# Layer 0's adaLN products in a two-layer fp32 diffusion step: half of the weight units as split fp32r products, loads spread over the phase, six units in flight in place of four

## The reference, cut to what matters

```python
def ada_modulate(x, cond, w_ada, b_ada, norm_g):
    mod = jax.nn.silu(cond) @ w_ada + b_ada
    shift, scale, gate = jnp.split(mod[:, None, :], 3, axis=-1)
    h = rms_norm(x, norm_g) * (1 + scale) + shift
    return h, gate
...
out, k, v = run_mixer(layer, h, ...)     # h @ w_in, attention and gating, @ w_out
x = x + gate * out
```

## Time and profile before

| | us |
|---|---|
| median of 3 runs | 2793.45 (2782.55 to 2796.37) |
| the profiled execution | 2779.65 |
| its span in the trace | 2778.1 |
| PE busy in the span | 2555.4 (92%) |
| DVE busy | 1720.0 (62%) |
| ACT busy | 809.4 (29%) |
| start of the first projection product | 165.56 |

### The profile page before, as it was taken

One profiled execution on the slowest core, in us unless ns is written; L12 is line 12 of the kernel. 1 busy time (PEld: TensorE's weight loads), 2 busy tenths in 40 slices (PEclk: granted clock), 3 DMA queues, 4 the chain that ended last, 5 costly groups with the idle time before them and its releaser, 6 DMA issues.

```text
span 2778.1 us, 38161 instructions
## 1 busy us (share of the span) xinstructions
PE 2555.4 (92%) x12040; PEld 2009.0 (72%) x12040; DVE 1720.0 (62%) x3165; ACT 809.4 (29%) x1698; POOL 428.1 (15%) x481
## 2 busy tenths in 40 slices
PE   7999999998898899979999989999999999998995
PEld 1258877777777678868877777777777778777884
DVE  1335788877887547766356555665656656555776
ACT  2012232322222222222233333333333333332221
POOL 0000212211222010000122212222222211101001
PEclk8999999999999999989999999999999999999998
DMA  7745544444544455644422222232222322237555
GB/s 273 253 148 163 192 147 144 137 152 157 171 158 147 164 187 194 216 152 148 131 91 89 86 78 83 86 98 92 68 91 88 99 87 95 84 122 241 189 194 203
DMA packets 165601, 395.42 MB, mean 142 GB/s; under 512 B 15008, under 2 KB 15648, under 8 KB 160992
## 3 DMA queue, kind: packets, MB, share of 16 engines
q1 hardware_dynamic: 132304, 249.08, 28.6%
q0 software_dynamic: 33168, 144.72, 14.8%
HBM read 332.93 MB, written 63.18 MB: 143 GB/s over the span
## 4 chain that ended last, share of the span: by engine, by line
PE 61%; DVE 19%; DVEq 8%; issue 5%; ACT 4%; DMA 2%; ACTq 0%; POOL 0%; SPq 0%; POOLq 0%
PE ps L554 46%; DVE w_lo L1138 4%; PE ps L440 3%; PE ps L449 3%; DVE small L1026 3%; PE ps L583 3%; PE ps L458 3%; DVEq L1161 2%; DVE work L1043 2%; ACT w_hi L769 1%; PE ps L541 1%; DMA w_raw<-in_w_ada_dram 1%; DVE wT_lo L1018 1%; DVEq L1024 1%; DVEq L1048 1%
## 5 line engine op out<-in xcount | busy, mean ns | idle before, releaser
L554 PE MATMUL ps<-w_hi,hT_hi 128*128 128x512 f32 x2800 | 1145.4, 409 | 15.0 <-DVE stage L1155 7.1
L554 PE MATMUL ps<-w_hi,hT_lo 128*128 128x512 f32 x2800 | 1106.4, 395 | 0.0
L554 PE MATMUL ps<-w_lo,hT_hi 128*128 128x512 f32 x2800 | 1100.7, 393 | 0.0
L1138 DVE TENSOR_TENSOR w_lo<-w_raw,w_hi 128x512 fp32r<-128x512 f32 x560 | 406.2, 726 | 351.7 <-ACT w_hi L769 333.8
L554 PEld LDWEIGHTS ps<-w_hi,hT_lo 128*128 128x128 f32 x2800 | 530.7, 190 | 118.9
L554 PEld LDWEIGHTS ps<-w_hi,hT_hi 128*128 128x128 f32 x2800 | 533.3, 190 | 112.0 <-issue 13.6
L554 PEld LDWEIGHTS ps<-w_lo,hT_hi 128*128 128x128 f32 x2800 | 533.2, 190 | 91.9 <-issue 1.9
L769 ACT CAST w_hi<-w_raw 128x512 fp32r<-128x512 f32 x560 | 346.6, 621 | 487.3 <-PE ps L554 468.5
L1168 DVE SCALAR_TENSOR_TENSOR ada_sum<-w_raw,cond,ada_sum 128x512 f32<-128x512 f32 x480 | 366.8, 805 | 35.8 <-issue 10.1
L720 ACT ACTIVATE work<-ps,small 128x640 f32<-128x640 f32 (+1 forms) x200 | 141.9, 710 | 594.5 <-DVE small L1029 594.4
L440 PE MATMUL ps<-consts,work 128*128 128x128 f32 x768 | 133.9, 289 | 68.9 <-DVE q_low_lo L1018 19.7
(11 more groups left out here) (185 smaller groups left out, 2374.1 us busy)
## 6 DMA issues: line engine op xcount, KB each, us to landing
w_raw<-in_w_in_dram SPq DMA_DIRECT2D x216, 512.0 KB, 3.9
w_raw<-in_w_ada_dram SPq DMA_DIRECT2D x256, 256.0 KB, 3.0
z<-stage POOLq DMA_DIRECT2D x27, 1280.0 KB, 5.1
w_raw<-in_w_ada_dram SPq DMA_DIRECT2D x64, 512.0 KB, 4.7
w_raw<-in_w_out_dram SPq DMA_DIRECT2D x64, 512.0 KB, 4.2
work<-z POOLq DMA_DIRECT2D x72, 320.0 KB, 3.7
work<-o POOLq DMA_DIRECT2D x8, 1280.0 KB, 7.7
x<-stage POOLq DMA_DIRECT2D x7, 1280.0 KB, 11.7
```

The costliest lines, as they stand in the source:

```text
L554: last = nc.tensor.matmul(ps[:, t, :], x[:, kt, t * P:(t + 1) * P], w[:, kt % RING, :], start=(kt == 0 and i == 0), stop=(kt == KT - 1 and ...
L1138: nc.vector.tensor_tensor(w_lo[:, kt % RING, :], w_raw[:, w_at(c, kt), kt % 2, :], w_hi[:, kt % RING, :].bitcast(F32), ALU.subtract).then_ ...
```

## The change

Of the 64 units, the even ones (`SPLIT`) are now handled as the projections' weights are: ACT rounds each of the two tiles to `w_hi`, DVE makes `w_lo`, and PE multiplies both with weights that hold, in four columns for each tile, the rounded value and the remainder of both conditions (`cst`, in the place of `wT_lo`). PE makes four single-pass fp32r matmuls of them in place of two plain fp32 ones. The odd units (`PLAIN`) stay plain fp32, with weights from `oT`. The weights are 128 columns wide for both, of which four are used; the rows of the result are added pairwise by `sel_col` in `ada0_finish`. Twenty of the plain units (`ADA_B`) get two new buffers, in the places of `ws_t` and of the two rotation tables, which are loaded after the last unit (`tables_in`). The blocks of `x` are issued after 1, 5, 8 and 11 plain units (`X_AFTER`), and ACT squares a block six units later. The feed of tiles 0 to 11 starts at units 34, 44 and 54 (`FEED_AT`), one tile for each two units, with the split of the next even unit between two tiles. Two of the w units come before the last ada unit, six behind it.

```diff
+X_AFTER = (2, 10, 16, 22)
+FEED_AT = (34, 44, 54)
+SPLIT = [u for u in range(N_ADA0) if u % 2 == 0]
...
-W_UNIT_AFTER = {56: (0,), 60: (1,), 62: (2,), 64: (3, 4, 5, 6, 7)}
+W_UNIT_AFTER = {63: (0, 1), 64: (2, 3, 4, 5, 6, 7)}
...
+ADA_B = [u for u in range(60) if u % 6 in (1, 3)]
+FIRST_A = [x for x in FIRST if x[0] == "w" or x[1] not in ADA_B]
...
+        spare = [at[:, :].rearrange("p (k n) -> p k n", n=NC) for at in (ws_t, tables)]
...
+            setup_at = {n: (n - 2,) for n in range(2, 11)}
             for n, (kind, u) in enumerate(FIRST):
...
+                if kind == "ada" and u in ADA_B:
+                    b = ADA_B.index(u)
+                    if b >= 2:
+                        sp.wait_ge(ada0_taken, PLAIN.index(ADA_B[b - 2]) + 1)
+                        sp.sem_inc(raw_taken, 1)
+                    dst, landed = spare[b % 2], spare_landed[b % 2]
+                else:
+                    at = FIRST_A.index((kind, u))
+                    if at >= RAW:
+                        held, v = FIRST_A[at - RAW]
+                        if held == "w":
+                            sp.wait_ge(w_lo_ready, C_L0 * KT + 2 * v + 2)
+                        elif v in SPLIT:
+                            sp.wait_ge(w_lo_ready, 2 * SPLIT.index(v) + 2)
+                        else:
+                            sp.wait_ge(ada0_taken, PLAIN.index(v) + 1)
...
-            sp.wait_ge(ada0_taken, N_ADA0)
+            sp.wait_ge(ada0_taken, len(PLAIN))
             sp.sem_inc(raw_taken, 1)
+            for dst, src in ((rope_c, a["rope"][0, 0]), (rope_s, a["rope"][0, 1]), (ws_t[:, :], a["spatial_weights"])):
+                sp.dma_start(dst, src).then_inc(tables_in, 16)
...
             def ada0_unit(u):
...
-                    last = nc.tensor.matmul(ps[0:2, m % 2, :], cond2[:, kt, :], w_raw[:, n % RAW, k, :],
-                                            start=(kt == 0), stop=(kt == KT - 1))
+                    if u in SPLIT:
+                        tile = 2 * SPLIT.index(u) + k
+                        pe.wait_ge(w_lo_ready, tile + 1)
+                        for w in (w_hi, w_lo):
+                            last = nc.tensor.matmul(ps[:, m % 2, :], cst[:, kt * 4:kt * 4 + P], w[:, tile % RING, :],
+                                                    start=(kt == 0 and w is w_hi), stop=False)
+                        last.then_inc(*((acc_ready, 5) if tile % KT == KT - 1 else (w_used, 1)))
+                    else:
+                        last = nc.tensor.matmul(ps[:, m % 2, :], oT[:, kt * 4:kt * 4 + P], ada0_buffer(u)[:, k, :],
+                                                start=False, stop=(kt == KT - 1))
...
-                    beside.setdefault(16 * b + 19 + x, []).append(("turn", 4 * b + x))
-            beside[62] = [("turn", 12)]
+                    beside.setdefault(FEED_AT[b] + 2 * x, []).append(("turn", 4 * b + x))
+            beside.setdefault(63, []).append(("turn", 12))
...
+            # ACT
+            for u in range(N_ADA0):
+                if u in SPLIT:
+                    split_ada(u)
+                if u - 6 in X_AFTER:
+                    square_block(X_AFTER.index(u - 6))
...
+                for b, at in enumerate(FEED_AT):
+                    if u - at in (1, 3, 5, 7):
+                        feed_hi(0, 4 * b + (u - at) // 2)
...
+            # DVE
+            for u in range(N_ADA0):
+                if u in SPLIT:
+                    split_ada(u)
+                if u % 8 == 0 and u > 0:
+                    ada0_row(u // 8 - 1)
+                if u == 31:
+                    dve.wait_ge(sq_done, 4 * TT)
+                    row_norms(partial=True)
+                    feed_block(0, 0)
...
+                if u in (21, 37, 53):
+                    ada0_columns((21, 37, 53).index(u))
+                for b, at in enumerate(FEED_AT):
+                    if u - at in (1, 3, 5, 7):
+                        feed_mid(0, 4 * b + (u - at) // 2)
+                        feed_lo(0, 4 * b + (u - at) // 2)
+                    if u - at == 9:
+                        feed_block(0, b + 1)
+            for kt in range(4):
+                split_lo(C_L0, kt)
+            ada0_row(7)
             ada0_columns(3)
...
+                wait(ada0_taken, X_AFTER[b] // 2)
```

More of the change, by code:

```diff
@@ L204, in kernel_program @@
         raw_taken = sem("raw_taken")
+        spare_landed = [sem(f"spare_landed{i}") for i in range(2)]
+        tables_in = sem("tables_in")
         ada_landed = [sem(f"ada_landed{i}") for i in range(ADA)]
@@ L406, in w_at @@
         def w_at(c, kt):
-            if isinstance(c, int) and c == 0:
+            if isinstance(c, int) and c == C_L0:
                 return W_AT[kt // 2] % RAW
@@ L831, in _, with split_ada, square_block @@
             act.sem_inc(S[1].s_exp, 1)
-            for b in range(4):
+            def split_ada(u):
+                wait_ada0_landed(act, u)
+                for k in range(2):
+                    tile = 2 * SPLIT.index(u) + k
+                    wait_slot_used(act, tile // KT, tile % KT)
+                    nc.scalar.copy(w_hi[:, tile % RING, :], ada0_buffer(u)[:, k, :]).then_inc(w_hi_ready, 1)
+            def square_block(b):
                 act.wait_ge(x0_in[b], 32)
@@ L1326, in _ @@
-            for b in range(3):
-                ada0_columns(b)
-                for kt in range(4 * b, 4 * b + 4):
-                    feed_mid(0, kt)
-                    feed_lo(0, kt)
-                feed_block(0, b + 1)
-                ada0_row(2 * b + 2)
-                if b == 2:
-                    for kt in range(4):
-                        split_lo(C_L0, kt)
-                ada0_row(2 * b + 3)
+            nc.vector.tensor_scalar(small[:, 32:64], small[:, 32:64], 0.5, None, ALU.mult)
@@ new lines, in _ @@
+            dve.drain()
+            parts = cst[:, 0:4 * KT].rearrange("p (k q) -> p k q", q=4)
+            for k in range(2):
+                x = small[:, 32 + 16 * k:48 + 16 * k]
+                nc.vector.tensor_copy(cond4[:, :, 2 * k], x)
+                nc.vector.tensor_copy(oT[:, 0:4 * KT].rearrange("p (k q) -> p k q", q=4)[:, :, 2 * k], x)
+                nc.vector.tensor_copy(parts[:, :, 2 * k], x)
+                dve.drain()
+                nc.vector.tensor_tensor(parts[:, :, 2 * k + 1], x, parts[:, :, 2 * k].bitcast(F32), ALU.subtract)
@@ new lines, in _, with split_ada, lambda_sums @@
+            dve.drain().then_inc(setup_dve, 1)
+            def split_ada(u):
+                for k in range(2):
+                    tile = 2 * SPLIT.index(u) + k
+                    dve.wait_ge(w_hi_ready, tile + 1)
+                    nc.vector.tensor_tensor(w_lo[:, tile % RING, :], ada0_buffer(u)[:, k, :],
+                                            w_hi[:, tile % RING, :].bitcast(F32), ALU.subtract).then_inc(w_lo_ready, 1)
+            def lambda_sums():
+                dve.wait_ge(setup_in, 16 * N_SETUP)
+                for k in range(2):
+                    nc.vector.tensor_tensor(lam4[:, 2 * k, :], lam4[:, 2 * k, :], lam4[:, 2 * k + 1, :], ALU.mult)
+                dve.drain()
+                nc.vector.tensor_reduce(small[:, 8:10], lam4[:, :, :].rearrange("p (a b) d -> p a b d", b=2)[:, :, 0, :],
+                                        AX_X, ALU.add)
+                nc.vector.tensor_scalar(gsub[:, :], gsub[:, :], 1.0 - LAMBDA_INIT, None, ALU.mult)
+                dve.drain().then_inc(setup_dve, 1)
@@ L1594, in _ @@
             load_v(L0, 0)
+            wait(tables_in, 16 * 3)
             rotate_head(L0, 0)
```

127 lines of the change are left out of this document (66 added, 61 removed).

## The result

The changed kernel takes 2767.8 us (median of 6 runs, 2762.1 to 2772.6) against 2791.6 us of the kernel before (median of 6, 2782.6 to 2796.4). The ratio is 0.992, with a 95% interval of 0.9904 to 0.9935: 24 us less, where 21.5 were forecast. The profiled execution took 2762.1 us, which is also the fastest of the six.

A forecast was written before the change was run, and what follows sets the result against it. PE was busy 92% of the span, so a shorter layer 0 adaLN phase should shorten the kernel: 77.5 + 42.8 + 23.8 = 144 us to the first projection product, against 165.6; 2793.45 - 21.5 = 2772 us, range 2752 to 2787.

The forecast's parts named there:

- The bound of the second half: After turn 0, DVE's feed chain plus splits was to bound the phase at 4.2 us for two units.
- the sum: Time to the first projection product: 77.5 + 42.8 + 23.8 = 144 us, in place of 165.6.
- Rival A: Second half: DVE is no bound, PE bounds it, three blocks take 54 us, start about 131 us; chance 0.12.
- The first half: Phase start to the end of turn 0 behind unit 33: bound by bytes, ending at 77.5 us.
- the landing of unit 28: First half: from bytes at 370 GB/s, unit 28 was to land at 59.9 us.
- the step: First half, unit 28's landing to DVE's end of split 30: two casts, five squares and remainders, 7.0 us.
- rival B: First half: six buffers do not fill the DMA or the clock falls at times; 8 to 14 us longer; chance 0.18.
- the 10.6 us behind split 30: End of first half: norms and scaling, split 32, PE's last products, unit 33, finish and turn 0, 10.6 us.
- Rival C: PE at the lower clock in the whole first half, start at 172 us, 2800 us; chance 0.06.
- The size: Whole kernel: 21.5 us less, from the earlier first projection product, giving 2772 us.
- three inefficiencies: adaLN phase: DMA full at the start, PE bound in the middle, neither at the end; the change touches all.
- the 44 waits of SP: SP's waits for PE's release of a buffer, 72.3 us in all, cited for PE bounding the phase's middle.

The follow-up runs named there:

- e4: Changed kernel with the next even unit's split moved between feed_mid and feed_lo on DVE, ahead of feed_hi on ACT; start 140.6 us, median 2761.3 us, ratio 0.9903.
- e1: Changed kernel with no unit split, all 64 plain fp32; start 141.2 us, median 2759.8 us, ratio 0.9893.
- e8: Changed kernel with splits only from unit 32 on, placed between feed_mid and feed_lo; start 134.6 us, median 2755.3 us, ratio 0.9879.
- e7: Changed kernel with all units plain and all of x issued at the start; start 153.0 us, median 2775.7 us, ratio 0.9953.
- e11: e8 with blocks of x issued after units 2, 8, 14 and 19, not 2, 10, 16 and 22; start 134.9 us, median 2753.2 us, ratio 0.9861.
- e10: Changed kernel with the split of unit 32 ahead of the norms on DVE; start 147.0 us, median 2762.8 us, ratio 0.9913.
- e9: e8 with the split of unit 32 ahead of the norms on DVE; start 138.1 us, median 2759.9 us, ratio 0.9898.

## Why the prediction was right, and where it was not

**The bound of the second half** held, place and size: 4.08 us for two units against 4.2, 66.1 us against 66.6, and e4 shows the cause, since filling DVE's wait for ACT took 9.5 us away. The nearness of the sum is in part luck: from the end of turn 0 to the end of turn 8 it took 40.8 us where the sum had 42.8, and from there to the start 25.3 where it had 23.8. Rival A had a chance only against this order, and e4's 56.6 us are near its 54.

**The first half** is the term that was mis-sized: turn 0 at 82.7 us, not 77.5. The first 2.8 us of this are the landing of unit 28. The sum took it from the bytes alone, 59.9 us. In the changed kernel its load could be issued only when split 22 had freed its buffer, and took 9.1 us beside the last block of `x`. DVE's row of split 22, SP's issue of the load, its row in the view of DMA issues (KB, us to landing), and ACT's casts of unit 28:

```profile
52.32 1.29 DVE L1393 TENSOR_TENSOR w_lo<-w_raw,w_hi 128x512 fp32r<-128x512 f32 x2 [3.50 <-ACT w_hi L890]
53.70 0.37 SPq L375 DMA_DIRECT2D w_raw<-in_w_ada_dram  x1
w_raw<-in_w_ada_dram SPq DMA_DIRECT2D x1, 512.0 KB, 9.1
62.82 1.14 ACT L890 CAST w_hi<-w_raw 128x512 fp32r<-128x512 f32 x2 [3.83 <-PE ps L628]
```

The last row names PE, but the place that this cast needs was free from 59 us, when PE had done the first tile of unit 24, and the load landed at 53.7 + 9.1 = 62.8 us. From there to the end of split 30 it took 6.9 us, and the step had 7.0. This is rival B's mechanism, loads that take 8 us and more in a full queue, at about half of its price.

The other 2.4 us: the 10.6 us behind split 30 were 13.0. The plain unit and the finish behind PE's wait took 3.28 and 1.16 us from start to start in place of 1.76 and 1.0, together 1.7 us, at a granted clock of 0.72 from 76 to 82 us. The small steps for the lambdas ahead of the norms, which the sum had left out, are 0.4 us. I had left the clock out of the sum and put it into the range.

Rival C is out, with clocks of 0.91 to 0.93. Between full and lower clock the length of a wait did not decide alone. Two waits of the changed kernel, and the plain unit behind each:

```profile
45.61 0.50 PE L628 MATMUL ps<-w_hi,wT_lo 128*128 128x512 f32 x1 [1.50 <-DVE w_lo L1393]
...
46.78 3.37 PE L632 MATMUL ps<-ws_t,oT 128*128 128x512 f32 x4
...
58.20 0.47 PE L628 MATMUL ps<-w_hi,wT_lo 128*128 128x512 f32 x1 [2.08 <-DVE w_lo L1393]
...
59.28 1.88 PE L632 MATMUL ps<-ws_t,oT 128*128 128x512 f32 x4
```

The forecast said that no row showed gaps shorter than 2 us. The earlier trace rows did: behind a wait of 0.98 us eight records took 3.60 us, which is full speed. The Trainium skill says that waits for data between bursts of products can throttle every burst anew (TensorE: Matmul & The Clock Gate, "HAM oscillation — how this bites in real kernels"). Its example is a kernel whose waits are longer than its bursts; here PE was busy for 21.4 of 26 and 16.2 of 20 us, so the forecast stretched the rule when it took the whole half to be at the lower level by it. Here some of the bursts behind waits ran at the lower clock, and not every one.

**The size** was met in the medians (24 us against 21.5) and not in the profile (16.8 us). A good part of the agreement is luck: the phase gave 5 us less than forecast, and the medians differ by 4 to 7 us more than the phase.

**What the gain comes from** was only half right. I listed three inefficiencies and priced the split first, as 27 us of PE work. e1 shows that in the order of the change this work was worth nothing: without the split the kernel is faster by 7 us, ratio 0.9893 in place of 0.9921 in the same comparison. It is worth something only in the second half and with e4's order: e8 starts 6.6 us ahead of e1. The gain is that of the buffers and, for plain units, of the loads' order. My rows had the sum for it: 113 us of plain units, 8 finishes and 13 turns are 130 us of 165.6. The other 35 us of the phase were the way of the first unit into the chip, waiting, and products at the lower clock, and they are more than the forecast gain. I did not work out the kernel without the split, and it was the rival that was missing. The new order of the w units and of the setup loads was not tried alone; it is in the 12.6 us that e7 has over the kernel before, together with the buffers and the later feed. The forecast also put the 44 waits of SP, 72.3 us, beside the stretch from 60 to 98 us; they are those of 60 to 170.

## What to carry to other kernels

Before work is moved from the engine that looks full, add up its work alone and set it against the stretch; if waiting makes up the difference, try buffers and the order of loads first. Here they brought more than less work did, and cost the other engines nothing. Where work moves to an engine that sits in a chain of short steps, look where in its order the new work stands: here it was nearly free inside a wait (3.37 us for two units) and added behind it (4.08 us). A long block of the same engine (norms, squares) stands in front of everything behind it, so bring its inputs earlier before moving single instructions around it: that took 1.8 us off turn 0 (e11 against e8), where moving one split took off 1.0 to 1.5 us (e10) or nothing (e9).

## What the runs showed of the hardware

A plain unit with 4 columns of weights and one with 128 took the same 1.88 us, and the granted clock was the same (0.93 and 0.91 in two stretches). After a wait of 2.0 us PE's clock sometimes fell and sometimes did not: unit 63 took 3.20 us in e11 and 1.98 in e8, nearly the same program. It could also fall behind a shorter one: a unit took 3.37 us behind 1.50 us of waiting. A landing of 512 KB into `w_raw` took 4.7 us at the median with the DMA at 241 GB/s (changed kernel, 60 to 145 us) and 8.3 us at 341 GB/s (0 to 60 us) with up to six units and a block of `x` under way. The forecast had 4.55 us for a load alone, and 8 us only in rival B.
